# Transposes of the attention probabilities at the head or in the middle of their weight unit

## What is computed

```python
for l in range(DEPTH):
    h = rms_norm(x, norm_mix[l])
    z = h @ w_in[l]
    qa, ka, va, qb, kb, vb, uc, gz = jnp.split(z, SPLIT_POINTS, axis=-1)
    ya = dense_gqa_blocked(rope(norm(qa)), rope(norm(ka)), va) @ w_branch_a[l]
    ob = weighted sum over groups of dilated_window_attention(qb, kb, vb)
    yb = ob @ w_branch_b[l]
    yc = multiscale_pool(uc, pool_lin[l], pool_scale[l]) @ w_branch_c[l]
    gates = jax.nn.sigmoid(gz + b_gate[l]).reshape(b, s, N_BRANCHES, D_MODEL)
    merged = gates[:, :, 0] * ya + gates[:, :, 1] * yb + gates[:, :, 2] * yc
    x = x + merged @ w_out[l]
    h2 = rms_norm(x, norm_ffn[l])
    x = x + (jax.nn.silu(h2 @ w_ffn_gate[l]) * (h2 @ w_ffn_up[l])) @ w_ffn_down[l]
```

## Time and profile before

| | |
|---|---|
| median of 3 runs | 861.21 us (860.22 to 861.93) |
| profiled execution, its own time | 861.18 us |
| its span in the profile | 859.4 us |
| PE busy | 842.9 us, 98% |
| weight loads (PEld) | 687.1 us, 80% |
| VectorE busy | 552.0 us, 64% |
| ScalarE busy | 419.6 us, 49% |
| GpSimd busy | 74.1 us, 9% |
| mean granted TensorE clock | 0.998 |

### The profile page before, as it was taken

The page is one execution under the profiler, slowest core; times in us unless marked ns, Lnnn a source line. Parts: engine busy times, 40 slices in busy tenths (PEclk is TensorE's granted clock), DMA queues, the critical chain, the costliest instruction groups (busy, mean ns, idle before and its releaser), DMA issues.

```text
span 859.4 us, 10421 instructions
## 1 busy us (share of the span) xinstructions
PE 842.9 (98%) x4060; PEld 687.1 (80%) x4068; DVE 552.0 (64%) x672; ACT 419.6 (49%) x505; POOL 74.1 (9%) x89
## 2 busy tenths in 40 slices
PE   4999999999999999999999999999999999999998
PEld 3788777878888888888888877878788888888886
DVE  3799556565876656564468985556576766566552
ACT  4665654455453444443446575443834544444340
POOL 2343000000002000000022420000000200000000
PEclk9999999999999999999999999999999999999999
DMA  8555434444547555555545543433454555555551
GB/s 327 210 183 195 147 117 154 172 147 148 191 153 240 195 176 174 189 196 195 180 170 194 191 153 142 170 131 141 148 196 170 193 195 186 170 185 192 196 184 61
DMA packets 22427, 151.59 MB, mean 176 GB/s; under 512 B 2624, under 2 KB 2800, under 8 KB 4848
## 3 DMA queue, kind: packets, MB, share of 16 engines
q1 hardware_dynamic: 20576, 144.25, 47.4%
q0 software_dynamic: 1808, 6.72, 2.3%
HBM read 149.91 MB, written 1.05 MB: 176 GB/s over the span
## 4 chain that ended last, share of the span: by engine, by line
PE 97%; DMA 2%; issue 0%; ACT 0%; SPq 0%; DVE 0%; ACTq 0%
PE bank L881 29%; PE bank L883 29%; PE bank L892 29%; PE bank L914 5%; PE bank L1025 2%; DMA w_raw<-in_stream_dram 2%; PE bank L1000 1%; PE bank L989 1%; PE bank L961 1%; PE bank L967 0%; PE bank L994 0%; ACT zvu L588 0%; DVE aT_lo L654 0%; ACT probsT L506 0%; SPq L386 0%
## 5 line engine op out<-in xcount | busy, mean ns | idle before, releaser
L621 DVE TENSOR_TENSOR w_lo<-w_raw,w_hi 128x2048 fp32r<-128x2048 f32 x134 | 306.3, 2288 | 130.9 <-ACT w_hi L484 130.6
L881 PE MATMUL bank<-w_hi,aT_hi 128*128 128x512 f32 x832 | 334.3, 402 | 6.8 <-ACT w_hi L480 4.9
L883 PE MATMUL bank<-w_hi,aT_lo 128*128 128x512 f32 x832 | 326.5, 392 | 0.0
L484 ACT ACTIVATE w_hi<-w_raw 128x2048 fp32r<-128x2048 f32 x134 | 256.3, 1913 | 106.1 <-DMA w_raw<-in_stream_dram 106.0
L892 PE MATMUL bank<-w_lo,aT_hi 128*128 128x512 f32 x832 | 224.2, 391 | 0.0
L881 PEld LDWEIGHTS bank<-w_hi,aT_hi 128*128 128x128 f32 x832 | 157.1, 189 | 43.4 <-issue 9.7
L892 PEld LDWEIGHTS bank<-w_lo,aT_hi 128*128 128x128 f32 x832 | 156.3, 188 | 33.2 <-DVE w_lo L627 0.2
L883 PEld LDWEIGHTS bank<-w_hi,aT_lo 128*128 128x128 f32 x832 | 157.3, 189 | 31.0
L881 PE MATMUL bank<-w_hi,hT_hi 128*128 128x512 f32 x176 | 68.9, 391 | 0.0
L883 PE MATMUL bank<-w_hi,hT_lo 128*128 128x512 f32 x176 | 68.5, 389 | 0.0
L499 ACT ACTIVATE hT_hi<-bank 128x512 fp32r<-128x512 f32 x22 | 13.2, 598 | 78.3 <-PE bank L914 78.3
(11 more groups left out here) (97 smaller groups left out, 704.0 us busy)
## 6 DMA issues: line engine op xcount, KB each, us to landing
w_raw<-in_stream_dram SPq DMA_DIRECT2D x136, 1024.0 KB, 4.7
bias_sb<-in_b_gate_dram POOLq DMA_DIRECT2D x12, 256.0 KB, 4.5
par<-in_params_dram POOLq DMA_DIRECT2D x3, 384.0 KB, 4.3
pool_mat<-in_pooling_dram POOLq DMA_DIRECT2D x1, 1024.0 KB, 8.3
out_dram<-x_sb SPq DMA_DIRECT2D x4, 256.0 KB, 4.0
x_sb<-in_x_dram SPq DMA_DIRECT2D x1, 512.0 KB, 3.7
x_sb<-in_x_dram POOLq DMA_DIRECT2D x1, 512.0 KB, 8.2
gates<-in_mask_dram POOLq DMA_DIRECT2D x1, 512.0 KB, 14.4
```

The source lines that it names most:

```text
L484: nc.scalar.activation(w_hi[:, j % RING, :, :].rearrange("p k n -> p (k n)"), w_raw[:, j % RING, :, :].rearrange("p k n -> p (k n)"), ACT. ...
L621: nc.vector.tensor_tensor(w[0], w[1], w[2].bitcast(F32), ALU.subtract).then_inc(unit_lo, 1)
L881: nc.tensor.matmul(o, src[0][:, k, tok], w_hi[:, slot, wk + i, :], start=first and i == 0, stop=False)
L883: nc.tensor.matmul(o, src[1][:, k, tok], w_hi[:, slot, wk + i, :], start=False, stop=False)
```

## The change

The probs batches leave the list of turns ahead of a unit and come first in the list of turns within it. For PE they so stand in the middle of units 12, 14, ..., 26, ahead of whatever was within these units already. ScalarE's pass keeps their copies ahead of the split, where they were, but the turns before the unit that are left (qk 6) come ahead of probs now. The order of the batches on banks 6 and 7 follows the lists and so changes in unit 14 alone. VectorE's pass skips probs in both lists.

```diff
--- before.py
+++ after.py
@@ -119,19 +119,20 @@
 
 
 def turns_before(t):
-    out = []
-    p = pair_at(t, 1)
-    if p is not None:
-        out += [("probs", 2 * p), ("probs", 2 * p + 1)]
-    out += TURNS_BEFORE.get(t, [])
+    out = list(TURNS_BEFORE.get(t, []))
     i, odd = divmod(t - U_FFN - 3, 2)
     if 0 <= i < FC and not odd:
         out.append(("hidden", i))
     return out
 
 
+def probs_within(t):
+    p = pair_at(t, 1)
+    return [] if p is None else [("probs", 2 * p), ("probs", 2 * p + 1)]
+
+
 def turns_within(t):
-    return TURNS_WITHIN.get(t, [])
+    return probs_within(t) + TURNS_WITHIN.get(t, [])
 
 
 
@@ -538,7 +539,7 @@
                 turn(BEFORE, ("mix_x", i))
             for lay in range(DEPTH):
                 for t in range(UNITS):
-                    for name in turns_before(t):
+                    for name in turns_before(t) + probs_within(t):
                         turn(lay, name)
                     if t == 0:
                         split_first(lay)
@@ -555,7 +556,7 @@
                             wait_emptied(act, lay, (f"z{Z_CHUNKS - 2 + n}", m))
                             nc.scalar.activation(gate_v3[:, m, :, n, :], gate_v3[:, m, :, n, :],
                                                  ACT.Sigmoid).then_inc(gate_done, 1)
-                    for name in turns_within(t):
+                    for name in TURNS_WITHIN.get(t, []):
                         turn(lay, name)
                     if t == 0:
                         for half in range(2):
```

## The result

The changed kernel takes 864.92 us (median; 863.91 to 866.08) against 861.20 for the kernel before in the same comparison (859.66 to 861.93). The ratio is 1.0046 with a 95% interval of 1.0033 to 1.0059: slower by 3.7 us, where 4.0 were forecast. The profiled execution has a span of 863.4 us, 4.0 above that of before.

What follows compares the result with a forecast made beforehand. TensorE (PE), busy 98% of the span, was taken to bound the kernel. From 861.18 us, PE's own changes added 3.1 and waits behind VectorE's delay 0.9, giving 865.2 us, range 862.6 to 867.8.

Steps and rivals of the forecast that it cites:

- The place is free: Transposes cost the same in a unit's middle as at its head; units 24 and 26 booked at 0.
- Three in a row hold the third by 0.49: A third transposed batch needs the first one's bank and waits 0.49 us for ScalarE's copy, with ScalarE idle.
- Unit 14, −0.15 each: Unit 14 keeps its groups, three now in the middle, and loses only 0.15 us of wait per layer: −0.3.
- Unit 12, +0.05 together: Unit 12: the wait for probs at the head goes, a bank wait replaces it: +0.05 us over both layers.
- Units 16 and 18, +0.42 each: Probs join the pool batch in the middle: −0.07 for one change saved, 0.49 bank wait; four times, +1.7 us.
- Units 20 and 22, +0.42 each for the bank: Same as units 16 and 18 but with the mixed batch: another +1.7 us over both layers.
- VectorE's lag, 0.9: VectorE 1.1 us later in odd units, so row 0 waits 0.05 at unit 22, 0.4 at 24: +0.9 over both layers.
- The clock: Rival 3: PE's clock falls in the new pauses, up to 5.44 us more per unit; one a layer gives 876; chance 2%.
- Rival 1's second half: No bank wait, but VectorE's delay grows to 1.6 and waits at 22 and 24 to some 1.5 a layer: 861.4; chance 7%.

Runs made afterwards that it cites:

- units 24 and 26 alone: Kernel before, with probs transposes moved to the middle in units 24 and 26 only: 861.05 us, ratio 1.0003.
- the doubled copy: Kernel after, with ScalarE reading the first of each two probs batches out twice before freeing its bank: 872.00 us, ratio 1.0126.
- the kernel with the copy doubled, before: Kernel before, with ScalarE reading the first of each two probs batches out twice before freeing its bank: 861.96 us, ratio 1.0014.
- the kernel with own banks: Kernel after, with the mixed batches of units 20 and 22 in banks 2 and 3: 864.94 us, ratio 1.0054.
- the lag removed: Kernel after, with ScalarE copying probs behind its split of unit t + 2: 863.77 us, ratio 1.004.
- a kernel that differs only in ScalarE's order: Kernel after, other batches at the head of units 12 to 22, probs copies behind ScalarE's split: 859.54 us; without the second edit 858.66.

## Why the prediction held, point by point

- *The place is free.* Right: units 24 and 26 alone, and the 6.35 of unit 26 in every kernel.
- *Three in a row hold the third by 0.49.* Right in mechanism and size: 1.29 from the transposes to L962 in the kernel after, so 0.50 of waiting, and the doubled copy adds 0.5 to the unit.
- *Unit 14, −0.15 each.* Measured 7.91 to 7.73, −0.18.
- *Unit 12, +0.05 together.* Measured 7.25 against 7.44 and 7.05, so +0.01 in the profiled pair. But the wait for probs at the head of unit 12 in layer 0, which I took as 0.60, is not the same in every execution: the kernel with the copy doubled, before, has none of it (6.81), and the one with units 24 and 26 alone has 7.37. The change itself could so bring up to 0.6 more than the +0.05, and I should have given the term that bound.
- *Units 16 and 18, +0.42 each.* Mis-sized: +0.54 and +0.48. In unit 16 the wait itself came as worked out. What is more is in the batch behind it: from the first pool product to the first product of row 1 it takes 123.43 − 121.79 = 1.64, and before it took 123.81 − 122.27 = 1.54. I took the joined batch at its old price. The first two rows are the pool batch before, the other two the mixed batch of unit 20 after:

```profile
122.27 1.89 PE L961 MATMUL bank<-pool_mat,zvu 128*128 128x256 f32 x8
123.81 0.58 PE L881 MATMUL bank<-w_hi,aT_hi 128*128 128x512 f32 x1
...
154.94 1.13 PE L968 MATMUL bank<-pooledT,par 128*128 128x256 f32 x4 [0.25 <-ACT probsT L507]
155.72 0.58 PE L882 MATMUL bank<-w_hi,aT_hi 128*128 128x512 f32 x1
```

 The mixed batch tells what the 0.10 goes with. It takes 155.72 − 154.94 = 0.78 after, where it waits behind the probs batches, but 155.01 − 154.33 = 0.68 in the kernel with own banks, where it stands at the same place and doesn't wait, and 0.67 before. So a batch that had to wait costs 0.1 beyond its wait. With the doubled copy the two batches take 1.64 and 0.78 still: the 0.1 did not grow with the wait. Why it is there the runs don't show.
- *Units 20 and 22, +0.42 each for the bank.* 7.25 to 7.71 is +0.46, and unit 22 is +0.52 with the gates' wait in it: 7.78 after, 7.75 with the lag removed. The same 0.1 behind the wait is in both.
- *VectorE's lag, 0.9.* The delay of the maxima was put at 1.1 and is 2.76 − 1.71 = 1.05. The waits came out as 0.03 at unit 22 and 0.35 at unit 24, 0.4 per layer and so 0.8. The mechanism is right; that the 0.35 comes so close to the 0.4 is in part luck. The prediction took 0.15 from VectorE's end to PE's product, while the rows that it names give 103.96 − 103.85 = 0.11. After, the first product of unit 24 starts 183.13 − 182.93 = 0.20 behind the end of unit 23, and the second 183.46 − 183.13 = 0.33 behind it, where 0.23 is usual: most of the rest is again what comes right behind a wait, and the sum had no term for it.
- *The clock.* It stays 1.00 over the new pauses, in the stretch around unit 16 and over units 21 to 23 of the kernel after (columns as in the earlier trace rows):

```profile
120.00:125.00 5.00, 4.75 (x25) 3.88 (x25) 0.94 (x1) 3.86 (x6) 0.00 (x0) 1.00 0.58 236
158.00:184.00 26.00, 25.57 (x150) 19.74 (x151) 18.59 (x25) 10.69 (x16) 0.54 (x1) 1.00 0.39 132
```

 Twelve pauses of 0.5 us did not move the clock here: it is 1.00 from 85 to 210 and from 500 to 640 us, where all of them lie. Nor did those of 1.0 with the doubled copy: there too it is 1.00 in both stretches, and each unit is 0.5 longer and no more. Pauses of this kind, between groups that go round PSUM banks, are what "TensorE: Matmul & The Clock Gate" of the Trainium skill warns of in its section "A second HAM failure mode: psum-queue depth-cycling". The traces here show no such swing of the clock.
- *Rival 1's second half.* Its reasoning, that a shorter middle gives its gain back as VectorE's lag, was a side remark. The own banks bear it out: units 20 and 22 are shorter by 0.48 and 0.47, units 21 and 24 longer by 0.45 and 0.52, net nothing. VectorE's delay grew to 1.5, where 1.6 was said. But the 0.45 at unit 21 is at a bank that the edit itself made two batches share, so the 1.5 a layer said for units 22 and 24 was not measured as such.

The sum in the touched units is +4.4 against +4.0 forecast, and the medians give +3.7. That the medians land within 0.3 of the forecast is therefore partly luck: the terms of units 16 to 22 were too small by about 0.6 together, the others too large by 0.2, and in the profiled pair the start, 1.2 shorter but begun 0.7 later, took 0.5 off again. The difference between the units and the medians is not settled: the start of the kernel, the same code in all, took from 22.3 to 25.9 us in the profiled executions, and what sets it was not tried.

## What to carry to other kernels

In a kernel like this one, whose busiest engine has no holes, moving work by itself cost nothing and brought nothing. What counts is which bank, and whose eviction, the neighbours of the new place need, so count how many batches in a row a rotation of banks can take before the first has to be copied out. Then follow the moved step on the in-order engines: a copy that waits for a later point holds everything queued behind it, and here that came back as a wait three steps on, at another bank. Work that stands at a head can also cover a late eviction, so ask what the first product behind it waits for once it is gone. That is an argument from the rows here (eight transposes take 0.79, the wait at unit 24 was 0.35); the late eviction with the transposes still at the head was not tried.

## What was not expected

The doubled copy in the kernel before left unit 12 of layer 0 at 6.81, where the kernel before shows 7.44 in its own profile: a wait for probs of 0.6 us came and went, ahead of any copy that the edit doubles. The trace shows how. Row 1 of unit 11 on PE, and VectorE's second tile of probs, in the kernel before with the copy doubled:

```profile
88.60 1.07 PE L894 MATMUL bank<-w_lo,aT_hi 128*128 128x512 f32 x4
...
89.08 0.62 DVE L748 TENSOR_SCALAR probs<-probs,rden 128x256 f32<-128x256 f32 x2
```

In this execution PE came out of the longer start 2.2 us later (30.72 against 28.52 at unit 1) and is still 88.60 − 86.43 = 2.2 later at unit 11. VectorE works without any idle from about 40 us to its probs, and ends them only 89.08 − 87.57 = 1.5 later. That difference of 0.7 covers the 0.6 that PE waited before. So what decides the wait at unit 12 is how far each of the two engines was set back at the start, ten units earlier.

And a kernel that differs only in ScalarE's order, with units equal to 0.04, had a median 0.9 us off over 11 and 12 runs. Below about 1 us, the lengths of single units in the trace say more of a change to this kernel than the medians.
